# Two normalisation roots, two pairs of operand splits and two output units in another order

## The reference, cut to what matters

```python
y_nsa = nsa_mixer(...)                       # attention, width 512
y_gmlp = gmlp_mixer(...)                     # width 256
y_conv = conformer_conv_mixer(...)           # width 256
y = concatenate([rms_norm(y_nsa, g_nsa), rms_norm(y_gmlp, g_gmlp), rms_norm(y_conv, g_conv)])
x = x + y @ w_out
...                                          # inside the cross attention:
p = softmax(einsum("bshd,bmhd->bhsm", q, k) * XATTN_HEAD_DIM ** -0.5)
o = einsum("bhsm,bmhd->bshd", p, v).reshape(b, s, D_MODEL)
return o @ wo
```

## Time and profile before

| | |
|---|---|
| median of three runs | 2493.0 us |
| the profiled execution's own time | 2493.11 us |
| its span, first to last instruction | 2490.7 us |
| PE busy | 2477.7 us, 99% |
| DVE busy | 1226.9 us, 49% |
| ACT busy | 919.9 us, 37% |
| POOL busy | 1258.6 us, 51% |
| granted TensorE clock | 0.999 of full speed |
| DMA traffic | 235.41 MB, mean 95 GB/s |

### The profile page before, as it was taken

The page is one execution under the profiler, slowest core; times in us unless marked ns, Lnnn a source line. Parts: engine busy times, 40 slices in busy tenths (PEclk is TensorE's granted clock), DMA queues, the critical chain, the costliest instruction groups (busy, mean ns, idle before and its releaser), DMA issues.

```text
span 2490.7 us, 34633 instructions
## 1 busy us (share of the span) xinstructions
PE 2477.7 (99%) x11970; PEld 2048.9 (82%) x11970; DVE 1226.9 (49%) x1439; ACT 919.9 (37%) x1333; POOL 1258.6 (51%) x882
## 2 busy tenths in 40 slices
PE   9999999999999999999999999999999999999998
PEld 8888888888888888888888888888877788888887
DVE  7444712553222542555135423227988855788363
ACT  5223523332222331335234322224367644444233
POOL 5554355555545545544455555555533443555455
PEclk9999999999999999999999999999999999999999
DMA  5332233333333333322333333336321232333332
GB/s 167 101 93 86 68 101 93 102 93 98 96 94 101 94 95 99 93 77 80 98 98 97 93 101 93 97 97 161 88 69 62 78 91 68 93 97 98 95 98 78
DMA packets 442029, 235.41 MB, mean 95 GB/s; under 512 B 16192, under 2 KB 436160, under 8 KB 441920
## 3 DMA queue, kind: packets, MB, share of 16 engines
q1 hardware_dynamic: 441488, 233.29, 32.4%
q10 hardware_dynamic: 432, 0.67, 0.1%
HBM read 231.84 MB, written 2.10 MB: 94 GB/s over the span
## 4 chain that ended last, share of the span: by engine, by line
PE 95%; DVE 4%; DMA 0%; issue 0%; POOL 0%; ACT 0%; DVEq 0%; SPq 0%; POOLq 0%
PE unit_ps L1901 63%; PE unit_ps L2057 13%; PE unit_ps L2043 8%; PE aux L1942 2%; DVE row L1481 1%; PE unit_ps L2433 1%; PE unit_ps L1942 1%; PE aux L2297 1%; PE o_banks L1942 1%; PE o_banks L1983 1%; PE aux L2345 1%; PE aux L2123 1%; PE unit_ps L2153 0%; PE aux L2366 0%; PE o_banks L1986 0%; PE aux L1972 0%
## 5 line engine op out<-in xcount | busy, mean ns | idle before, releaser
L495 POOL TENSOR_TENSOR wl<-raw,wh 128x512 fp32r<-128x512 f32 x860 | 1246.6, 1470 | 1212.2 <-ACT wh L578 816.6
L578 ACT ACTIVATE wh<-raw 128x1024 fp32r<-128x1024 f32 x304 | 322.6, 1061 | 1029.6 <-PE unit_ps L1901 975.6
L1901 PE MATMUL unit_ps<-ah,wh 128*128 128x512 f32 x1280 | 501.3, 392 | 0.0
L1901 PE MATMUL unit_ps<-ah,wl 128*128 128x512 f32 x1280 | 498.1, 389 | 0.0
L1901 PE MATMUL unit_ps<-al,wh 128*128 128x512 f32 x1280 | 498.0, 389 | 0.0
L1901 PE MATMUL unit_ps<-bh,wh 128*128 128x512 f32 x768 | 299.8, 390 | 0.0
L1901 PE MATMUL unit_ps<-bh,wl 128*128 128x512 f32 x768 | 298.8, 389 | 0.0
L1901 PE MATMUL unit_ps<-bl,wh 128*128 128x512 f32 x768 | 298.8, 389 | 0.0
L1901 PEld LDWEIGHTS unit_ps<-al,wh 128*128 128x128 f32 x1280 | 240.3, 188 | 50.1 <-issue 0.5
L1901 PEld LDWEIGHTS unit_ps<-ah,wl 128*128 128x128 f32 x1280 | 240.2, 188 | 50.0
L1901 PEld LDWEIGHTS unit_ps<-ah,wh 128*128 128x128 f32 x1280 | 240.3, 188 | 49.9 <-issue 0.5
(11 more groups left out here) (420 smaller groups left out, 3873.9 us busy)
## 6 DMA issues: line engine op xcount, KB each, us to landing
raw<-w_in_dram SPq DMA_DIRECT2D x143, 512.0 KB, 4.0
raw<-w_up_dram SPq DMA_DIRECT2D x64, 512.0 KB, 4.0
raw<-w_down_dram SPq DMA_DIRECT2D x64, 512.0 KB, 4.1
raw<-up_dram SPq DMA_DIRECT2D x44, 512.0 KB, 3.8
raw<-w_conv_out_dram SPq DMA_DIRECT2D x16, 512.0 KB, 4.1
raw<-w_ret_out_dram SPq DMA_DIRECT2D x16, 512.0 KB, 4.1
raw<-w_o_dram SPq DMA_DIRECT2D x16, 512.0 KB, 4.1
raw<-down_dram SPq DMA_DIRECT2D x16, 512.0 KB, 3.9
```

What stands on the lines that cost most here:

```text
L495: last = pool.tensor_tensor(wl[j][:, half], raw[j % 2][:, half], wh[j][:, half].bitcast(F32), ALU.subtract)
L578: act.activation(wh[j][:], raw[j % 2][:], ACT.Copy).then_inc(w_hi, 1)
L1901: last = pe.matmul(unit_ps[j % 2][:], w[j][:, k], v[:, k * T:(k + 1) * T], start=(k == 0 and n == 0), stop=(k == KB - 1 and n == 2))
```

## The change

It has three parts.

1. On ACT the square root of the first mixer (part_r[1]) leaves step 6 and stands in step 10, just ahead of the second's. On DVE the two reciprocals that use them stand one step later each: the first in step 11, the second in step 12.
2. On ACT part_hi(0), part_hi(1) move from the end of step 12 into step 13, and part_hi(2), part_hi(3) from the end of step 13 into step 14, each pair behind weigh and ahead of the third exponential.
3. On PE blocks 6 and 7 of the first two XO units are taken unit by unit: XO + 0 is finished ahead of the last blocks of XO + 1.

```diff
 mixer_norms on ACT
                 if k == CV_STEP + 1:
                     act.wait_ge(mean_out, 3)
                     act.activation(part_r[2], part_r[2], ACT.Sqrt, bias=eps[:, 0:1]).then_inc(cv_std, 1)
-                    act.activation(part_r[1], part_r[1], ACT.Sqrt, bias=eps[:, 0:1]).then_inc(part_std, 1)
...
                 elif k == CV_STEP + 5:
                     act.wait_ge(mean_out, 4)
+                    act.activation(part_r[1], part_r[1], ACT.Sqrt, bias=eps[:, 0:1]).then_inc(part_std, 1)
                     act.activation(part_r[2], part_r[2], ACT.Sqrt, bias=eps[:, 0:1]).then_inc(part_std, 1)
...
                         weigh(k)
+                        if k in (GM_PARTS + 1, CV_PARTS + 1):
+                            for part in range(2):
+                                part_hi((0 if k == GM_PARTS + 1 else 2) + part)
...
-                if k in (GM_PARTS, CV_PARTS):
-                    for n in range(2):
-                        part_hi((0 if k == GM_PARTS else 2) + n)
                 mixer_norms(k)
...
 mixer_norms on DVE
                     square_sum(part_src)
-                elif k == CV_STEP + 5:
+                elif k == CV_STEP + 6:
                     root_inverse(1, part_r[1])
-                elif k == CV_STEP + 6:
+                elif k == CV_STEP + 7:
                     root_inverse(2, part_r[2])
...
-            for k in (6, 7):
-                pe.wait_ge(in_lo, IL + k + 1)
-                for f in range(2):
+            for f in range(2):
+                for k in (6, 7):
+                    if f == 0:
+                        pe.wait_ge(in_lo, IL + k + 1)
                     last = xo_part(f, (k,))
-                    if k == KB - 1:
-                        last.then_inc(mm, 1)
+                last.then_inc(mm, 1)
```

## The result

| | before | changed |
|---|---|---|
| median of 17 runs | 2493.09 us (2492.71 to 2493.72) | 2497.93 us (2497.60 to 2499.39) |
| profiled execution, span | 2493.11, 2490.7 us | 2498.56, 2496.1 us |

The ratio is 1.0020, with a 95% interval of 1.0014 to 1.0027: slower, by 4.84 us in the medians, where the forecast said 3.6. The interval is clear of no change, and the chances said "the same" with 97%. The mean granted clock of the span was 0.999 in every execution of the kernel before whose clock was recorded; of the 17 of the changed kernel five had 0.997, eight 0.998 and four 0.999, and the five with 0.997 are among the slowest seven.

The account below looks back on a forecast made before the run. PE bounds the kernel (chain 95% PE), with DVE, ACT, PE in step 14 without slack. 0.75 for step 7 + 3.35 for steps 13 and 14 - 0.5 for XO = 3.6 us: 2496.6 us, range 2494.3 to 2498.0.

Parts of the forecast that it names:

- the same: Whole kernel: time changes by less than 0.2%, 5 us; chance 97%, against 2% slower and 1% faster.
- The signs named in advance: Changed profile: late DVE maximum, PE idle before step 14's second scores, longer step 10 wait, slower L1585, no seam idle.
- Step 7: Earlier POOL collides with DVE's L1585; DVE ends later, PE's step 10 wait grows: +0.75 us, bounds 0 and +1.05.
- Root in step 10: One more ACT activation in step 10 makes the following copy, PE and POOL late: +0.45 us, bounds 0 and +0.62.
- Reciprocal: Step 12 on DVE: 3.35 us added ahead of step 14's maximum, less 0.89 and 0.35 given back: +2.1 us.
- Halves: Step 14: two ACT operations ahead of the third exponential delay PE's second scores, +1.15 us; the copy's wait goes, -0.4.
- The 0.5 held in reserve for step 15: Later pair of halves between step 15's exponentials: priced 0, with 0.5 us reserved because ACT and DVE will be late.
- XO: Seam after XO: first unit's last product starts earlier, so PE's idle time goes: -0.5 us, bounds -0.3 and -0.6.
- Steps 13 and 14 together ... 3.35: Sum for steps 13 and 14: 2.6 plus 1.15 is 3.75 us later, less 0.4 at the copy, is 3.35.
- an idle time of 3 us or more: Step 14: PE's second pair of scores idle for 3 us or more, released by ACT.
- Rival 3: Steps 14 and 15: shifted POOL meets the weighing's small products, PE's transposes wait: +1.0 to +1.5 us, 2497.6 to 2498.1; 12%.

Follow-up runs that it names:

- e7: Changed kernel plus one unused ACT copy in step 7, holding POOL back; median 2497.59 us, +4.5 over the kernel before.
- e5: Kernel before with the XO order and only the second mixer's pair of upper halves moved; median 2492.63 us, -0.4 over before.
- e2: Kernel before with only the two pairs of upper halves (part_hi) moved; median 2493.52 us, +0.5 over before.
- e4b: Changed kernel plus 2 and 4 dummy products on PE ahead of step 14's two pairs of scores; median 2496.74 us, +3.7 over before.
- e3: Kernel before with only the XO order changed; median 2492.53 us, -0.5 over before.
- e6: Kernel before with only the two reciprocals moved one step later, square roots left in step 6; median 2496.35 us, +3.3 over before.
- e8: Changed kernel with the first mixer's pair of upper halves put back ahead of the weighing; median 2496.63 us, +3.6 over before.
- e1: Kernel before with only the square root and the two reciprocals moved; median 2497.16 us, +4.1 over before.
- e11: Kernel before plus one unused square root on ACT in step 13, making PE stand idle before step 14's second pair; median 2497.18 us, +3.9.

## Why the prediction came out as it did

**What bounds the kernel, and the mechanism: right.** DVE, then ACT, then PE in step 14, without slack. The signs named in advance are in the profile, save two: PE's idle time in step 14 came in two pieces, 1.07 and 2.05 us, and its wait for DVE in step 10 did not grow (0.35 us, where 0.5 to 1.3 was named). The stretch that the text ahead calls full is not so everywhere: from 1870 to 1880 us DVE is busy for 5.7 us only, outside the steps that the change touches.

**Step 7: right in the collision, wrong in the path to PE.** +0.75 forecast. PE's product at step 10 was 0.69 us late, of which 0.15 had come from before the step (1901.29 and 1901.44 for its first transposed product), so 0.54. The collision is as forecast, and e7 shows it by taking it away. But PE didn't lose the time in a longer wait in step 10: DVE's late maximum reached it by way of ACT, in the wait of 0.76 us at 1908.43. DVE came to step 10 as late as PE did, so the two paths cost the same here.

**Root in step 10: right.** +0.45; the copy moved from 1927.89 to 1929.03, 1.14 us with the 0.69 it brought along.

**Reciprocal: right in kind, 2.1 too low by 0.4.** The maximum came 3.68 us late, 2.54 after step 10's 1.14. L1338 gave back its 0.89 (0.75 us instead of 1.64); the 0.35 I took from the idle time before the maximum was not given: the row still has 0.46 there.

**Halves: 1.15 forecast, 1.03 measured; more than the 0.4 at the copy was won.** From the second pair to the first output unit it is 0.85 us: 0.47 at the copy and 0.36 at the transposes behind it (L2216), ahead of which PE stood idle for 0.20 us before. The 0.5 held in reserve for step 15 without a place is the give-back that e5 shows; e2 pays it as well (its lag grows from 0.13 to 0.41 us from the first output unit to 1968.80), and so does e4b (0.29).

**XO: right.** -0.5; e3 gives -0.51.

**The step that failed: "Steps 13 and 14 together ... 3.35".** The sum carries a standstill of PE at its own length alone and puts what follows it at nothing. What came on top, 1.2 us in the medians and 2.2 in the profiled execution, is the granted clock: at 0.50 from 1947.1 to 1953.9, 5 us of it with PE at work. With PE kept at work instead, e4b gives +3.67 for the 3.6 forecast. That agreement is in part luck, since the terms were off both ways. As measured they are 0.54 for step 7, 0.45 for step 10, 2.54 for the reciprocal and 1.03 for the halves, less 0.85 won in step 14, plus 0.29 given back in step 15, less 0.47 at the seam: 3.5 us by the traces.

I had foretold an idle time of 3 us or more. The trace of before has no wait of PE over 1.2 us between its products, but it does have a row on a longer idle time, at its very end, which the forecast does not use. PE's last products and the windows behind them:

```profile
2481.34 1.39 PE L2440 MATMUL aux<-d,mean_d 128*128 128x256 f32 x4
```

```profile
2484.00:2485.00 1.00, 0.00 (x0) 0.00 (x0) 0.97 (x2) 0.00 (x0) 0.65 (x1) 1.00 1.04 349
2485.00:2486.00 1.00, 0.00 (x0) 0.00 (x0) 0.86 (x3) 0.00 (x0) 1.00 (x3) 0.54 0.37 123
```

PE's work ends at 2482.73 and the clock falls at 2485.1, 2.4 us later; no product follows there, so it costs nothing. That should have been a term with a bound, as long as PE takes to come back, and a rival of its own. Rival 3 reached 2498 by another mechanism, which isn't there: the product of the weighing took 0.99 us in step 14, but no wait came of it.

**The chances.** I counted 5 us as what a measurement can tell from none. The 17 runs of each kernel do better: the change's interval, 3.5 to 6.7 us, is clear of zero while its middle sits at my bound. 2% on slower was too little: the forecast of +3.6 had an own range up to +5.4, and nothing in it stood for what its idle time would bring with it. The range's low end, +1.5, also left out the low bounds of two terms (1.1 for the halves, -0.6 for XO); with them it is +1.3. That the time fell within the range at all is the width of its other terms, not a term for the clock.

## What to carry to other kernels

A standstill of TensorE costs its length, and in some executions also the time at half clock behind it: here two idle times of 1 us were enough in e6 and e8, and not in e1's profiled execution. When a forecast contains such an idle time, give the clock a term of its own with a bound, and test it by filling the wait with products that nobody needs. Read the effect from the stretch behind the wait, where it stands clear of what the filling itself costs. Two moves that depend on each other (a root and its reciprocal) are to be priced together, since each alone can cost nearly as much as both. A small wait that goes away, like the one at the copy of step 14, is won only if the next meeting of the engines has room; here it was given back some 10 us later.

## What the runs showed that was not expected

- The moment of the clock's fall differs. In the changed kernel it came 0.2 us into the second idle time (2.05 us), in e7, with the same two, at the end of the second; in e11 2.7 us into a single one of 2.82; in e6 and e8, with two of about 1 us, 0.5 and 0.9 us after PE had resumed; in e1, with the same two as e8, not at all. What decides it is not shown by these runs: the length of one idle time is not enough to tell. The same program differs by up to 3.2 us between executions (e11).
- Products in fp32 with 256 columns appear as two records each and took 0.47 to 0.50 us each, so the first fill was twice too long.
- A copy of 0.45 us more on ScalarE in step 7, which delayed the weight's rounding by 0.31 us, made the kernel's step shorter by 0.55 us (e7).
